# Differential attention's turn and multiply moved one item later, with a fourth buffer of scores

## What is computed

```python
s = jnp.einsum('bhpid,bhpjd->bhpij', qi, kt) + bias[None, :, None]
p = jax.nn.softmax(s, axis=-1)
a = p[:, :, 0] - lam * p[:, :, 1]
return jnp.einsum('bhij,bhjv->bhiv', a, vt)
```

## Time and profile before

| | us |
|---|---|
| timed runs | 2035.66, 2035.91, 2039.91 |
| median | 2035.91 |
| the profiled execution, its own time | 2039.57 |
| its span from first to last instruction | 2038.1 |
| PE busy in the span | 1994.8 |
| PE idle in the span | 43.3 |

### The profile page before, as it was taken

How to read it: one execution, slowest core, us unless ns; L and a number is a source line. 1 busy time by engine, 2 the same in 40 slices (tenths; PEclk the granted TensorE clock), 3 DMA queues, 4 the chain that set the end, 5 groups by cost and what they waited for, 6 DMA issues and landing times.

```text
span 2038.1 us, 23795 instructions
## 1 busy us (share of the span) xinstructions
PE 1994.8 (98%) x9219; PEld 1615.7 (79%) x9219; DVE 1221.6 (60%) x2182; ACT 709.2 (35%) x1000; POOL 842.8 (41%) x563
## 2 busy tenths in 40 slices
PE   8998999999999999999999999999999999999999
PEld 6776788888888766888888878888888877787787
DVE  4465442299999543222223588888888865885434
ACT  3333542323333333322323333333333335344531
POOL 0000000005888888877600677777777302300000
PEclk9999999999999999999999999999999999999999
DMA  6433232146666656966647799999999912221132
GB/s 218 166 124 123 85 142 96 64 138 156 144 149 139 134 113 146 273 148 147 164 159 256 250 375 360 376 355 374 354 370 376 354 32 73 73 83 52 32 103 83
DMA packets 176272, 374.92 MB, mean 184 GB/s; under 512 B 57632, under 2 KB 90912, under 8 KB 164640
## 3 DMA queue, kind: packets, MB, share of 16 engines
q1 hardware_dynamic: 109248, 277.03, 39.7%
q0 software_dynamic: 61696, 84.12, 15.4%
q10 hardware_dynamic: 5216, 12.26, 1.6%
HBM read 312.38 MB, written 60.95 MB: 183 GB/s over the span
## 4 chain that ended last, share of the span: by engine, by line
PE 90%; DVE 6%; ACT 3%; issue 1%; DMA 0%; ACTq 0%; DVEq 0%
PE bank L1489 34%; PE bank L303 16%; PE bank L305 16%; PE bank L304 16%; PE bank L393 1%; PE bank L2092 1%; PE bank L1125 1%; PE bank L1379 1%; PE bank L2118 1%; DVE weights_low L296 1%; PE bank L2138 1%; ACT weights_high L287 0%; PE bank L508 0%; DVE mix_small L834 0%; DVE u_low L1540 0%
## 5 line engine op out<-in xcount | busy, mean ns | idle before, releaser
L1352 POOL DMA_INDIRECT gates_scratch<-slot_gate,slot_place x256 | 437.9, 1711 | 303.1 <-DVE slot_place L1320 205.6
L1489 PE MATMUL bank<-xn_low,u_high 128*128 128x512 f32 x1024 | 409.9, 400 | 0.0
L1489 PE MATMUL bank<-xn_high,u_low 128*128 128x512 f32 x1024 | 399.4, 390 | 0.0
L1489 PE MATMUL bank<-xn_high,u_high 128*128 128x512 f32 x1024 | 398.7, 389 | 0.0
L1540 DVE TENSOR_TENSOR u_low<-u_raw,u_high 128x1024 fp32r<-128x1024 f32 x128 | 156.3, 1222 | 311.2 <-ACT u_high L1511 310.9
L303 PE MATMUL bank<-v_high,w_high 128*128 128x512 f32 x768 | 299.1, 389 | 1.3 <-DVE v_low L1744 1.3
L304 PE MATMUL bank<-v_low,w_high 128*128 128x512 f32 x768 | 298.9, 389 | 0.0
L305 PE MATMUL bank<-v_high,w_low 128*128 128x512 f32 x768 | 298.9, 389 | 0.0
L296 DVE TENSOR_TENSOR weights_low<-weights_raw,weights_high 128x1024 fp32r<-128x1024 f32 (+1 forms) x105 | 127.5, 1217 | 214.0 <-ACT weights_high L287 213.4
L1635 POOL DMA_INDIRECT row_unit<-units_scratch,slot_place x128 | 170.1, 1329 | 156.2 <-DMA units_scratch<-hidden 117.5
L1628 POOL DMA_INDIRECT row<-in_peer_v,row_places x128 | 191.1, 1493 | 85.4 <-DVE x L1755 51.9
(11 more groups left out here) (340 smaller groups left out, 3058.1 us busy)
## 6 DMA issues: line engine op xcount, KB each, us to landing
u_raw<-in_peer_u SPq DMA_DIRECT2D x128, 512.0 KB, 4.0
v_raw<-in_peer_v SPq DMA_DIRECT2D x64, 1024.0 KB, 7.1
weights_raw<-in_w_in SPq DMA_DIRECT2D x64, 512.0 KB, 3.7
hidden_scratch<-hidden SPq DMA_DIRECT2D x128, 192.0 KB
hidden_in<-hidden_scratch SPq DMA_DIRECT2D x32, 768.0 KB, 11.6
gates_scratch<-nothing POOLq DMA_DIRECT2D x16, 1024.0 KB, 4.1
gate_in<-gates_scratch SPq DMA_DIRECT2D x32, 512.0 KB, 7.9
weights_raw<-in_w_out SPq DMA_DIRECT2D x16, 512.0 KB, 3.7
```

The source lines that it names most:

```text
L1352: pool.engine.indirect_dma_start(gates, bass.IndirectOffsetOnAxis(p.slot_place[t][:, i:i + 1], 0), p.slot_gate[t][:, i:i + 1], None, compu ...
L1489: step = pe.engine.matmul(m.bank[b][:, :], left[:, k, :], right[:, k, :], start=(done == 0), stop=(done == 3 * KT - 1))
```

## The change

`diff_scores` gets a fourth buffer and the items take them by i % 4 (`weigh_columns`, the small columns for maximum, sum and share, likewise). In round i of `attention()` there now stand score(i), then multiply(i - 4) and weigh(i - 3), then subtract(i - 1), on all three engines, and there is one round more. DVE's score(i) waits for the turning of item i - 4, since that had the buffer before. To make room, `nothing` is halved, and POOL clears the same bytes with 32 DMAs of 512 KB, each behind four increments of `multiplied`.

```diff
+        self.scores.append(region.tensor("diff_scores3", [P, 2, T], F32))
...
     def weigh_columns(self, i):
-        base = 32 + 8 * (i % 3)
+        base = 24 + 8 * (i % 4)
...
     def attention():
-        for i in range(len(DIFF_ITEMS) + 3):
+        for i in range(len(DIFF_ITEMS) + 4):
             if i < len(DIFF_ITEMS):
                 score(i)
                 yield
+            if 0 <= i - 4 < len(DIFF_ITEMS):
+                multiply(i - 4)
             if 0 <= i - 3 < len(DIFF_ITEMS):
-                multiply(i - 3)
-            if 0 <= i - 2 < len(DIFF_ITEMS):
-                weigh(i - 2)
+                weigh(i - 3)
                 yield
             if 0 <= i - 1 < len(DIFF_ITEMS):
                 yield
...
-            if 0 <= i - 3 < len(DIFF_ITEMS) and DIFF_ITEMS[i - 3][1] == TT - 1:
-                h = DIFF_ITEMS[i - 3][0]
-                act.wait_ge(s.diff_multiplied, i - 3 + 1)
+            if 0 <= i - 4 < len(DIFF_ITEMS) and DIFF_ITEMS[i - 4][1] == TT - 1:
+                h = DIFF_ITEMS[i - 4][0]
+                act.wait_ge(s.diff_multiplied, i - 4 + 1)
...
-            if 0 <= i - 2 < len(DIFF_ITEMS):
-                w = i - 2
+            if 0 <= i - 3 < len(DIFF_ITEMS):
+                w = i - 3
...
-            if i >= 3:
-                dve.wait_ge(s.diff_turned, i - 2)
+            if i >= 4:
+                dve.wait_ge(s.diff_turned, i - 3)
...
-CLEARED, CLEARINGS = 2048, 16
+CLEARED, CLEARINGS = 1024, 32
...
-        pool.wait_ge(s.multiplied, 8 * (i + 1))
+        pool.wait_ge(s.multiplied, 4 * (i + 1))
```

More of the change, by code:

```diff
@@ L516, in weigh @@
         for j in range(t + 1):
-            step = pe.engine.transpose(m.bank[6][:, j * P:j * P + P], b.scores[i % 3][:, 0, j * P:j * P + P], ident)
+            step = pe.engine.transpose(m.bank[6][:, j * P:j * P + P], b.scores[i % 4][:, 0, j * P:j * P + P], ident)
         step.then_inc(s.diff_turned, 1)
@@ L677, in attention @@
                 n = (t + 1) * P
-                scores, (top, total, share) = b.scores[i % 3], b.weigh_columns(i)
+                scores, (top, total, share) = b.scores[i % 4], b.weigh_columns(i)
                 act.wait_ge(s.diff_negated, i + 1)
```

## The result

| | us |
|---|---|
| before, median of six runs (lowest, highest) | 2035.86 (2035.66, 2039.91) |
| after, median of six runs (lowest, highest) | 2026.41 (2025.52, 2027.25) |
| ratio, with its 95% interval | 0.9943 (0.9933 to 0.9953) |
| profiled execution, before and after, own time | 2039.57 and 2025.52 |
| spans of these two | 2038.1 and 2024.2 |

What follows compares the result with a forecast made beforehand. PE was taken as the bound, busy 1994.8 of 2038.1 us, with 13.3 us in attention waits and clock falls; -9.04 - 4.26 + 3.0 = -10.3 from 2035.91 gave 2025.6, stated as 2026, range 2022 to 2032.

Steps and rivals of the forecast that it cites:

- The four waits: PE's waits at weigh(2), (6), (10) and (14) for subtract, 9.04 us together, all counted as gone.
- What is late next: Attention: ACT's copies late for multiply(0), (4) and (12), new PE waits of 3.0 us, bounds 0 and about 6.
- DVE's lateness at score(14): DVE's start on item 14's scores put 1.0 us late, so its exponentials start 3.4 us after PE's scores.
- PE's side: PE's work from the end of item 14's scores until it comes to multiply(12), put at 12.1 us.
- The waits at multiply(0) and (4): New PE waits for ACT's copies in the attention, put at 0.5 us for multiply(0) and 1.0 for multiply(4).
- The falls of the clock: Three falls of PE's clock behind waits of 1.89, 2.70 and 3.43 us, put at 4.26 us and expected gone.
- -10.3: Forecast net change in us, -9.04 - 4.26 + 3.0, taken from the median of 2035.91 to give 2026.
- Rival B: Attention's waits go but the clock gives nothing, only 6.0 us won, 2029.9 us; chance 0.3.
- The late stages: Stages after the attention, said to hold no waits of PE of the size of the attention's four.
- Costs of nothing: POOL's 16 more DMAs, 8.5 us on a waiting queue, and the retention's unchanged small waits, said to cost nothing.
- C: Attention's waits move to L529 almost in full, 9 us, net gain 0 to 4; 2033.5 us, chance 0.13.
- D: Slower: ACT's late copy delays its splitting, DVE's next score and the next copy in the attention; 2042 us, chance 0.04.

Runs made afterwards that it cites:

- split_behind: Kernel before, with DVE's low part of a chunk moved behind the chunk's first step in the attention's three groups; 2024.53 us, ratio 0.9938; second run 2024.02 us, 0.9932.
- buffer_only: Kernel before with the smaller clearings and the fourth buffer of scores, but weigh(i - 2) and multiply(i - 3) left in place; ratio 1.0000.
- before_again: Kernel before, unchanged, run once more; six executions took 2035.05 to 2035.43 us, five took 2039.62 to 2040.88.
- clear_only: Kernel before with only the clearing changed, 32 DMAs of 512 KB instead of 16 of 1 MB; ratio 1.0001.
- move_only: Kernel after's order but three buffers of scores, DVE's score(i) waiting for item i - 3; 2033.78 us median, ratio 0.9979.

## Why the prediction was right, point by point

**The four waits.** Right: 9.04 us at the transposes went to none, by the mechanism named, subtract behind a splitting behind the longest exponentials. `split_behind` shows it by itself, `buffer_only` shows that the buffer is no part of it. The kernel after does two things to these waits: it asks for the item later, and, since score and subtract stand one slot earlier, it puts the splitting behind subtract(2), (6), (10) and (14). How much of the 9.04 us either would have taken by itself is not shown.

**What is late next.** Right in place, too high in price. The waits came at multiply(0), (4) and (12) and not at (8), as laid out, but with 0.42, 0.32 and 0.48 us instead of 0.5, 1.0 and 1.5. The step that failed is one term of the last of them, DVE's lateness at score(14). These rows of the timelines of PE, DVE and ACT in the kernel after show it:

```profile
163.31 1.45 PE L509 MATMUL bank<-diff_k,diff_q 128*128 128x384 f32 x4
```

```profile
164.97 1.01 DVE L831 SCALAR_TENSOR_TENSOR diff_scores<-alibi_sb,bank 128x384 f32<-128x384 f32 x2
```

```profile
167.21 0.62 ACT L682 ACTIVATE diff_scores<-diff_scores,mix_small 128x384 f32<-128x384 f32 x1 [4.07 <-DVE mix_small L837]
...
177.03 0.26 ACT L697 ACTIVATE diff_turned<-bank 128x128 f32<-128x128 f32 x1
```

PE's scores of item 14 end at 163.31 + 1.30 = 164.61 (the 1.30 of the earlier trace rows). DVE starts on them at 164.97, 0.4 us late and not 1.0, and the exponentials begin at 167.21, 2.6 us after the scores and not 3.4. The other parts held: from there to the copy's end I had 10.2 us, and it took 177.29 - 167.21 = 10.1; PE's side I had at 12.1 us, and PE was there at 177.34 - 0.48 = 176.86, after 12.25. So 0.8 of the 1.0 us of error is DVE's lateness, which I had estimated and not laid out instruction by instruction like the rest. The waits at multiply(0) and (4) I had built on the same estimate; only that of multiply(0) was near.

**The falls of the clock.** The step that failed here is that I took the three falls of the profile from a median that had fewer. In the profiled execution they cost 4.91 us, not 4.26, and went; with 9.04 and 1.2 of new waits that is the 12.7 of the stretch. The four executions near 2035.8 that set the median were of the lower level, and `before_again` at that level had one fall, 1.7 us. The sum for it is then -9.4 - 1.7 + 1.2 = -9.9, which is what the stretches differ by (110.40 - 100.50); 9.45 was measured between the medians. That my -10.3 came so near is luck: falls 2.6 us too high, new waits 1.8 too high and old waits 0.4 too low cancelled. That the median was a lower one is luck too, since the ratio has 11.6 us. Rival B, which took the levels of the timed runs from the falls, was right about the larger part of their difference. It was wrong about the sum, since it had no fall at all in the median and new waits of 3.0; with one fall and 1.2 it would have said 2035.91 - 9.4 - 1.7 + 1.2 = 2026. The Trainium skill (TensorE: Matmul & The Clock Gate, Part 1, What's actually happening) says that the gate's count runs freely, and that the same kernel therefore shows more or fewer slow matmuls at its start from run to run. These runs show such a difference in the middle of a kernel: the waits of 1.9 and 2.7 us set off a fall in one execution and none in another, the wait of 3.43 in both. The count itself no run here shows.

**The late stages.** I wrote that they have nothing of this size, and by totals that is so. But the trace of before has there the wait of 2.7 us of L303 with a fall behind it, about as long as the second longest wait of the attention, and I did not see it. It is in the kernel after as well, so it cost the forecast nothing.

**Costs of nothing.** Right: the clearings (`clear_only`), and the retention, whose waits for `ret_weights` are 1.8 and 1.0 us in both kernels, and whose first matmul stands 1838.0 us before the span's end in both.

**C and D.** The waits did move to L529 in `move_only`; the buffer prevents it in the kernel after. D did not show in any kernel; none was slower than the kernel before, and its loop was not tried by itself.

## What to carry to other kernels

Where one engine waits for another's result in a pipeline, look first at what stands ahead of that result in the other's queue, and whether it is needed as soon: here a chunk's splitting, needed two chunks later, stood in front of a subtract needed at once, and moving that one instruction behind the first step gave more than an extra buffer and a whole item of distance. If distance is added, buffer and schedule have to be deepened together; here the one alone gave nothing and the other somewhat over a third. And before subtracting a sum made on one profile from a median, see whether the profiled execution stands at the median's level, and by what it differs.

## What the runs showed of the hardware

The price of a long wait is not the wait alone, and it is not the same in each execution. In the four profiles with the order of before (`clear_only` and `buffer_only` among them), TensorE's clock fell to the lower level behind the waits of 1.9 and 2.7 us in three and stayed in the fourth, behind 3.4 us it fell in all four, behind 1.0 and 1.5 us in none. In `move_only` it fell behind 1.8 and 2.9 us and not behind 1.7. Late in the second block it fell behind a wait of 2.7 us in eleven of twelve profiles. A fall of the order of before cost 1.6 to 1.7 us of PE's busy time, and one in `move_only` lasted about twice as long.

The kernel before has two groups of times, from 2034.6 to 2035.9 and from 2037.9 to 2040.9 us, with waits that are the same to 0.4 us in a profile of each; the kernel after, without long waits in the attention, has one, 2025.5 to 2027.3. Taking long waits out thus gains more in the slower executions than in the faster, and narrows the spread. What decides whether such a wait sets off a fall in a given execution, no run here shows.
